# Attention in a two-layer hybrid backbone step: values as weights with two heads on the two halves of the columns, and the softmax sums divided by a diagonal while the probabilities are turned

## What is computed

```python
def block(args):
    qn_i, qr_i = args
    s = jnp.einsum('bqhd,bkhd->bhqk', qn_i, kn) + jnp.einsum('bqhr,bkr->bhqk', qr_i, kr)
    p = jax.nn.softmax(s.astype(jnp.float32) * scale, axis=-1).astype(v.dtype)
    return jnp.einsum('bhqk,bkhd->bqhd', p, v)
```

```python
u = jnp.take(u_tab, i_i, axis=0)
a = jax.nn.gelu(jnp.einsum('td,thkd->thk', x_i, u))
return jnp.einsum('thk,thkd->td', a * g_i, jnp.take(v_tab, i_i, axis=0))
```

## Time and profile before

| | us |
|---|---|
| median of 3 runs | 4947.24 (4945.59 to 4952.51) |
| the profiled execution | 4941.85 |
| its span in the trace | 4939.7 |
| TensorE busy | 3914.8 (79%) |
| VectorE busy | 3459.5 (70%) |
| ScalarE busy | 868.6 (18%) |
| GpSimd busy | 1660.4 (34%) |
| attention of "p", layer 0 | about 160 to 204 |
| attention of "s", layer 0 | about 626 to 744 |
| attention of "p", layer 1, among V | about 1829 to 1936 |
| attention of "s", layer 1 | about 2944 to 3058 |

### The profile page before, as it was taken

One profiled execution on the slowest core, in us unless ns is written; L12 is line 12 of the kernel. 1 busy time (PEld: TensorE's weight loads), 2 busy tenths in 40 slices (PEclk: granted clock), 3 DMA queues, 4 the chain that ended last, 5 costly groups with the idle time before them and its releaser, 6 DMA issues.

```text
span 4939.7 us, 40296 instructions
## 1 busy us (share of the span) xinstructions
PE 3914.8 (79%) x12034; PEld 1996.6 (40%) x12034; DVE 3459.5 (70%) x9184; ACT 868.6 (18%) x2434; POOL 1660.4 (34%) x1437
## 2 busy tenths in 40 slices
PE   7888789697988866767867579799797777777776
PEld 3437464345433333323533246445442333232322
DVE  0333788857888867777677878877787777766665
ACT  1221241001111112211111123100111111111111
POOL 0230132332233334444433323224134444443432
PEclk9879899899999988889989789999999889999999
DMA  7325377765699999999999766767479999999998
GB/s 269 117 80 197 144 273 264 268 259 214 249 376 421 407 366 402 412 409 398 417 414 421 290 231 249 300 231 274 169 266 396 406 413 411 405 415 421 417 421 347
DMA packets 223333, 1585.71 MB, mean 321 GB/s; under 512 B 26678, under 2 KB 29026, under 8 KB 32012
## 3 DMA queue, kind: packets, MB, share of 16 engines
q0 software_dynamic: 186784, 1354.97, 68.5%
q1 hardware_dynamic: 36332, 228.18, 12.0%
HBM read 1571.74 MB, written 11.30 MB: 320 GB/s over the span
## 4 chain that ended last, share of the span: by engine, by line
PE 37%; DMA 29%; DVE 22%; issue 6%; ACT 3%; POOL 3%; SPq 0%; DVEq 0%; ACTq 0%; POOLq 0%
DMA sb_gbufs<-in_peer_uv,sb_idx 16%; PE ps L1105 13%; DMA sb_arena<-in_peer_uv,sb_idx 11%; PE ps L1004 7%; DVE sb_gbufs L1863 5%; PE ps L1042 3%; DVE sb_arena L1863 3%; DVE sb_eacc L1886 2%; PE ps L674 2%; PE ps L719 2%; PE ps L688 2%; POOL sb_gbufs L2106 1%; PE ps L1022 1%; PE ps L862 1%; PE ps L1075 1%
## 5 line engine op out<-in xcount | busy, mean ns | idle before, releaser
L2106 POOL DMA_INDIRECT sb_gbufs<-in_peer_uv,sb_idx x768 | 940.5, 1225 | 1864.4 <-PE ps L1105 826.8
L1105 PE MATMUL ps<-sb_arena,sb_dge 128*128 128x512 f32 x1856 | 925.2, 649 | 301.6 <-ACT sb_dge L1368 301.4
L1105 PE MATMUL ps<-sb_gbufs,sb_dge 128*128 128x512 f32 x1856 | 907.6, 638 | 304.8 <-ACT sb_dge L1368 304.7
L2106 POOL DMA_INDIRECT sb_arena<-in_peer_uv,sb_idx x512 | 563.8, 1101 | 869.3 <-PE ps L1105 830.9
L1863 DVE CUSTOM_DVE_ANT_0 sb_gbufs<-sb_gbufs,sb_keep 128x1024 f32<-128x1024 f32 x512 | 621.4, 1226 | 289.5 <-DMA sb_gbufs<-in_peer_uv,sb_idx 288.0
L1863 DVE CUSTOM_DVE_ANT_0 sb_arena<-sb_arena,sb_keep 128x1024 f32<-128x1024 f32 x512 | 619.5, 1223 | 262.8 <-DMA sb_arena<-in_peer_uv,sb_idx 261.3
L1105 PEld LDWEIGHTS ps<-sb_arena,sb_dge 128*128 128x128 f32 x1856 | 367.9, 206 | 821.5 <-ACT sb_dge L1368 421.6
L1105 PEld LDWEIGHTS ps<-sb_gbufs,sb_dge 128*128 128x128 f32 x1856 | 362.4, 203 | 814.3 <-issue 426.7
L1363 ACT ACTIVATE sb_small<-sb_small 128x2 f32<-128x2 f32 x512 | 104.0, 203 | 2182.4 <-DVE sb_small L1874 2182.4
L1886 DVE SCALAR_TENSOR_TENSOR sb_eacc<-sb_gbufs,sb_small,sb_eacc 128x1024 f32<-128x1024 f32 x299 | 388.2, 1298 | 9.2 <-DVE sb_small L1897 0.3
L1368 ACT ACTIVATE sb_dge<-sb_ident,sb_small 128x128 f32<-128x128 f32 x928 | 327.3, 395 | 122.5 <-DVE sb_small L1960 121.8
(11 more groups left out here) (257 smaller groups left out, 4307.6 us busy)
## 6 DMA issues: line engine op xcount, KB each, us to landing
sb_ring<-in_w_ada SPq DMA_DIRECT2D x48, 1024.0 KB, 8.9
sb_ring<-in_w_wq SPq DMA_DIRECT2D x32, 1024.0 KB, 6.3
sb_ring<-in_w_hy SPq DMA_DIRECT2D x24, 1024.0 KB, 7.5
sb_ring<-in_w_ga SPq DMA_DIRECT2D x16, 1024.0 KB, 8.0
sb_ring<-in_w_gb SPq DMA_DIRECT2D x16, 1024.0 KB, 9.5
sb_ring<-in_w_oab SPq DMA_DIRECT2D x16, 1024.0 KB, 7.8
sb_ring<-in_w_out SPq DMA_DIRECT2D x14, 1024.0 KB, 9.0
sb_gbufs<-in_peer_uv,sb_idx POOLq DMA_INDIRECT x768, 11.0
```

The lines of the kernel that those rows point to most:

```text
L1105: q = pe.matmul(ps[:, c, :], dge[:, b, :], gbuf[b][:, D + c * 512:D + c * 512 + 512], start=(h == 0 and i == 0), stop=(h == HALVES - 1 and ...
L2106: nc.gpsimd.indirect_dma_start(out=gbuf[b], out_offset=None, in_=I["peer_uv"], in_offset=bass.IndirectOffsetOnAxis(ap=idx[:, col:col + 1], ...
```

## The change

The diagonal. For each head VectorE takes the reciprocal of the row sums and multiplies the identity by it (`inverse_sums`, in `rdiag`, two buffers). TensorE multiplies `prob`, as weights, by this diagonal instead of transposing it: the product is the turned probabilities, divided already. `normalise` goes. `inverse_sums(i-1)` stands at the start of VectorE's step i, ahead of the maximum of head i, and TensorE's turning(i-1) waits for it (semaphore `rd` instead of `prob`).

The values as weights. Two heads are multiplied at every second step: 64 value columns of each as weights, the turned probabilities (128 columns) moving, the even head's result on PSUM partitions 0 to 63 and the odd one's on 64 to 127. The result stands turned, so the four blocks are copied to `attnT` by ScalarE straight from the bank (`heads_done`), and the turning at L841 and its copy go. `probT` has four buffers instead of two.

The pace of a head step is 4.0 instead of 4.5. The E units that stand among the 32 head steps of "s" fall from 54 to 49 in layer 0 and from 50 to 46 in layer 1; of the nine, two go ahead of the attention, and of the seven behind it three stand among the gate products (L1004).

```diff
-        at = [20 * k] + [10] * nt + [15] + [8] * nt + [8, 10] + [4.5] * (NH * nt) + [10] + [8 * k + 2] * (8 if self.latent else 12)
+        at = [20 * k] + [10] * nt + [15] + [8] * nt + [8, 10] + [4.0] * (NH * nt) + [10] + [8 * k + 2] * (8 if self.latent else 12)
...
                         m.then_inc(s["s_ps"], 1)
+                    if i >= 3 and i % 2:
+                        j, h = (i - 3) // NH, (i - 3) % NH
+                        b = g.head_bank(j)
+                        if h == 0:
+                            claim(b, *at("aT", j + 1))
+                        pe.wait_ge(*at("pT", i - 1))
+                        for kt in range(g.nk):
+                            for u in (0, 1):
+                                m = pe.matmul(ps[64 * u:64 * u + VD, b, h * 64:h * 64 + 128], v.V[:, kt, (h + u) * VD:(h + u + 1) * VD],
+                                              v.probT[:, (i - 3 + u) % 4, kt * 128:kt * 128 + 128],
+                                              start=(kt == 0), stop=(kt == g.nk - 1), skip_group_check=True)
+                        m.then_inc(s["o_ps"], 1)
                     if 1 <= i <= N:
-                        pe.wait_ge(*at("prob", i))
+                        pe.wait_ge(*at("rd", i))
                         claim(4, *at("pT", i))
                         for kt in range(g.nk):
-                            m = pe.transpose(psf[:, 4 * 512 + kt * 128:4 * 512 + kt * 128 + 128],
-                                             v.prob[:, (i - 1) % 2, kt * 128:kt * 128 + 128], ident[:, :])
+                            m = pe.matmul(psf[:, 4 * 512 + kt * 128:4 * 512 + kt * 128 + 128], v.prob[:, (i - 1) % 2, kt * 128:kt * 128 + 128],
+                                          v.rdiag[:, (i - 1) % 2, :], start=True, stop=True)
                         m.then_inc(s["trp"], 1)
-                    if i >= 2:
...
                 vacate()
-                for j in range(nt):
-                    claim(g.lo(j), *at("aT", j + 1))
-                    pe.wait_ge(*at("attn", j + 1))
...
+                def heads_done(j):
+                    act.wait_ge(*at("o_ps", NH // 2 * (j + 1)))
+                    act.activation(v.attnT[:, :, j * 128:j * 128 + 128], ps[:, g.head_bank(j), :].rearrange("p (c t) -> p c t", c=4), ACT.Copy).then_inc(s["aT"], 1)
...
-                def normalise(j):
...
+                def inverse_sums(i):
+                    dve.wait_ge(*at("prob", i + 1))
+                    if i >= 2:
+                        dve.wait_ge(*at("trp", i - 1))
+                    link(dve.reciprocal(ssum[:, 32 + i % 2:33 + i % 2], ssum[:, i:i + 1]))
+                    dve.tensor_scalar(v.rdiag[:, i % 2, :], ident[:, :], ssum[:, 32 + i % 2:33 + i % 2], None, ALU.mult).then_inc(s["rd"], 1)
 
                 for i in range(nt * NH):
+                    if i:
+                        inverse_sums(i - 1)
                     dve.wait_ge(*at("s_ps", i + 1))
```

47 lines of the change are left out of this document (13 added, 34 removed).

## The result

| | before | after |
|---|---|---|
| median, first comparison (4 runs each) | 4949.33 us | 4994.26 us (4990.45 to 5007.05) |
| ratio, first comparison | | 1.0096, 95% interval 1.0075 to 1.0116 |
| median, second comparison (14 and 5 runs) | 4949.79 us | 4995.19 us (4983.79 to 5005.71) |
| ratio, second comparison | | 1.0080, 95% interval 1.0067 to 1.0094 |
| profiled execution, its span | 4941.85, 4939.7 us | 4990.45, 4988.6 us |

The change costs 45 us. Forecast were 4965 and a range of 4943 to 4990. The direction was right; the size is two and a half times the +18 of the forecast, and the row of rival 2 (+43, 4990) is the nearest. The page of the kernel after: PE 3924.7 us busy (before 3914.8), DVE 3484.7 (3459.5), ACT 869.5 (868.6). TensorE has 10 us more work and VectorE 25.

A forecast was written before the change was run, and what follows sets the result against it. VectorE was taken to bound the attention of "s", strict engine order phase 0, DMA phase 1. "s" 2 x (3.4 + 2.2 + 3 - 3) = +11.2, phase 0 +6, phase 1 +2: +19, 4961 profiled, 4965 median; range 4943 to 4990.

The forecast's parts named there:

- rival 2: Each stall in phase 1 costs DMA time, 26 us (seven at 3.7) instead of 2: +43, 4990; chance 0.13.
- Phase 1: Attention of "p" among V: turning waits for VectorE's next head step, V's matmuls 6.9 us later, seven times; +2 us.
- So I take +2: one loss at the first stall: Phase 1: queued gathers cover later stalls, so delays don't add up; +2 us, bounds 0 and 34.
- The moved units: Nine E units leave the head steps of "s": -0.23 and -0.18 us per step, +2.2 us a layer elsewhere.
- VectorE sets the pace there, and E units are what fills it: Attention of "s" before the change: VectorE's counted step, 3.38 and 3.19 us, matches the measured paces.
- three land among the gate products, where TensorE is busy for 186 of 200 us and VectorE for 141: free: Three of the nine moved units cost nothing; half of the other six count, +2.2 us a layer.
- VectorE's step in "s": Inverse adds 0.42 us, `normalise` and units go: 3.46 and 3.33 us a head step, +3.4 us a layer.
- forecast 2.2 us a pair: TensorE in "s": 20 value instructions one behind the other at 0.11 us, nothing gained; a step is 3.33 us.
- Rival 1: Column halves run side by side, values of "s" take 1.1 us a pair: +8 us, 4955; chance 0.27.
- The bound of 5 us a layer on the changes of weight width: TensorE in "s": 32 changes between full-width and 64-column weights a layer cost at most 5 us.
- The end of "s": Last maximum to convolution: 12.8 us becomes 10.6 or 8.5 at the half clock; -3 us a layer taken.
- Phase 0: Attention of "p": inverse and turning stand before F's matmuls, +0.8 us at six places, +1 at the end; +6 us.

The follow-up runs named there:

- before_pace: The kernel before with the pace of a head step at 4.0, nothing of the attention changed: 4964.41 us, ratio 1.0025.
- pace_back: The changed kernel with the pace of a head step at 4.5 again: 4977.49 us, ratio 1.0044.
- both_back: The changed kernel with inverses of "p" in VectorE's own step and the pace at 4.5: 4949.28 us, ratio 1.0002.
- p_own_step: The changed kernel with the inverse of "p" made in VectorE's own step, right behind the same head's maximum: 4973.05 us, ratio 1.0039.
- late_s_new: both_back with 5 and 4 E units moved from ahead of the h2 step to behind it: 4935.35 us, ratio 0.9967.
- att45_rest40: p_own_step with E units dealt as by pace 4.5 in the attention of "s", as by 4.0 elsewhere: 4971.22 us, ratio 1.0047.
- both_no_inverse: both_back without inverse and diagonal in "s" (division left out), turning by the constant identity: 4942.77 us, ratio 0.9990.
- both_transposes: both_no_inverse with the turning of "s" as 5 transposes instead of 5 products of two passes: 4938.94 us, ratio 0.9978.
- both_in_turn: both_back with a pair's value instructions one head after the other instead of alternating: 4964.31 us, ratio 1.0038.
- att40_rest45: p_own_step with E units as by pace 4.0 in the attention of "s", 4.5 elsewhere, leftovers in the following convolution: 4959.59 us, ratio 1.0024.
- before_pace50: The kernel before with the pace of a head step at 5.0: 4959.02 us, ratio 1.0016.

## Why the prediction was wrong, step by step

**Phase 1 (forecast +2 us, measured +12 in the trace and 15 to 16 in the medians).** The place and the cause of the waits were seen rightly, their length less so: 6.9 us each were expected, the trace has 8 of 38.6 us in all, 4.8 on average, the longest 9.2. What failed is the sentence "So I take +2: one loss at the first stall", with the reason that the queue before the DMA is short once and then stays so. The windows show the contrary: the DMA is back at 420 to 424 GB/s after a stall and falls again with the next, 12.6 us in all, so each of seven costs about 1.8 us of transfer. Rival 2 had it that each stall costs; its 3.7 us each are twice the measured, and its condition, a queue that doesn't refill, was not measured. TensorE's granted clock in 1841 to 1941 is 0.78 (0.89 before), which rival 2 named too; no run separates what it adds. The bounds (0 to 34) held; with 12.6 in place of 2 the forecast would have been 4976.

**The moved units (forecast -8 us in all, measured +15 by before_pace and +17 by pace_back).** The forecast has them in two terms: -0.23 and -0.18 us in VectorE's step, which is 12.7 us for 31 steps in two layers, and +2.2 us a layer for where they go. Three things failed. First, "VectorE sets the pace there, and E units are what fills it": in before_pace the steps take 3.33 and 3.28 us against 3.36 and 3.23, so nothing came back. In the new attention it was 0.16 and 0.12 (from pace_back to the change), 0.13 and 0.00 (from both_back to p_own_step). Second, "three land among the gate products, where TensorE is busy for 186 of 200 us and VectorE for 141: free": VectorE's mean share says nothing on who is late at the end of the stretch. That is the h2 step, where TensorE waited 21.6 us for VectorE already, and this wait isn't in the prediction. Units taken from ahead of it give time back (late_s_new). Third, a pace is no count of nine: it deals all 260 units anew, and att45_rest40 shows that the arrangement outside the attention alone makes the h2 wait 29.4 us. With +15 in place of -8 beside the 12.6 of phase 1 the forecast would have come out at 4999, near the 4994 measured.

**VectorE's step in "s" (forecast 3.46 and 3.33 us, measured by the scores 3.53 and 3.56).** The inverse was right to 0.02 us. With the units of before (both_back) the step grows by 0.34 and 0.30 us, forecast 0.31. What was missing is the gain from fewer units, above. both_no_inverse and both_transposes show that a step is neither VectorE's nor TensorE's alone: each shortens it.

**TensorE (forecast 2.2 us a pair, measured 1.31).** Rival 1 was right on the mechanism and wrong in its sum, because the terms for phase 1 (it has 0) and for the units were the ones that failed. TensorE's time isn't free in the new step either: 0.35 us a step more cost 15 us in both_in_turn, of which the steps show 11. The bound of 5 us a layer on the changes of weight width held; what they cost is in the last section.

**The end of "s" (forecast -3 us, measured -6.0 in layer 0 and -4.8 in layer 1).** The chain of waits after the change, from the last maximum to the convolution:

```profile
739.51 0.82 DVE sb_nmax L1565
740.33 1.19 DVE sb_eacc L1884
741.63 0.30 DVE sb_arena L1556
741.98 1.38 PE ps L832 x10
743.38 0.71 ACT sb_arena L1192
744.14 1.34 PE ps L824 x20
745.50 0.61 ACT sb_keep L1196
746.11 0.24 issue
746.35 5.82 PE ps L857 x13
```

6.8 us instead of 12.8. In layer 0 the steps are those of the forecast, but the forecast took the clock over from the old end, where it was granted at half, 1.2 GHz. Windows of the change and then of before (the seventh figure is the granted clock):

```profile
740.00:746.30 6.30, 3.71 (x40) 3.10 (x38) 4.63 (x12) 2.87 (x6) 1.35 (x2) 1.00 0.81 300
...
735.00:740.00 5.00, 4.25 (x21) 4.07 (x20) 0.67 (x2) 0.70 (x1) 0.00 (x0) 0.50 0.82 326
```

At 2.4 GHz and on the two halves in turn 20 value products take 1.34 us, where they took 4.17. TensorE's busy share in the attention ahead is the same, 86% in both. What differs just ahead of the fall is a wait: before, TensorE stood idle for 2.2 us until 733.79, with the clock at 0.87 from 730 to 735 and at 0.50 after; in the change no wait from 733 to 746 is longer than 0.95 us, and the clock stays at 1.00. Whether that is why wasn't tested.

**Phase 0 (forecast +6 us).** F's matmuls start 0.77 us after its last VectorE step (0.95 forecast):

```profile
190.12 0.68 DVE L1475 TENSOR_TENSOR sb_gbufs<-ps,sb_gbufs 128x512 f32<-128x512 f32 x1
...
191.57 3.60 PE L687 MATMUL ps<-sb_arena,sb_gbufs 128*128 128x512 f32 x8
```

From 160 to 200 the trace falls back by 7.9 us (2.1 to 10.0), within the 4 to 8 of the forecast. By 400 it is only 1.2 us late, but that is no cover for the delay: p_own_step, which has no such delay, gains as much in that stretch and is 8.9 us ahead of the kernel before at 450. Something in the new kernel gains 7 to 9 us there that the forecast doesn't have; no run isolates it. p_own_step is 10 to 11 us ahead of the change from 400 to 740. Of these, 7 go between 740 and 820, where its waits for ScalarE at L687 and for VectorE at L889 are each 2 us longer, and 1 to 4 are left from there to phase 1. The medians say 6.5.

**What stays open.** The arrangement of the units makes the h2 waits longer (7.5 and 7.9 us of the change's 45), but by what step, when their number hardly changes, isn't shown. Nor are the single steps of the 10 us between 3100 and 3450, which come in pieces of 3 to 5 us at waits for L1594, for a weight and at the gates; att45_rest40 shows them too, so they belong to the arrangement. Why 5.0 costs the new attention 30 us and the old one 8 stays open; only the head steps were measured (3.79 and 3.26 us in before_pace50). What the new attention of "p" gains between 200 and 400 is open too.

## What to carry to other kernels

Where engines run a list in different orders, ask for each new wait in which piece of the other engine's own order the releaser stands; a wait that crosses such an offset can cost up to a whole piece each time, and the stretch bound by DMA paid here for every one of them, not once. Filler work isn't free because its engine has a low busy share: here it was on the path ahead of the next wait for that engine, and moving it across the longest such wait gave 14 to 18 us. When a change carries a retuned number along, time the number alone first; here it was a third of the loss.

## What was not expected of the hardware

Products on the two halves of the columns, alternating: 20 instructions (64-column weights, 128 moving columns, float32) in 1.31 us; the same with ten for one half and then ten for the other: 2.02 us. Where full-width weights follow 64-column ones (L824 to L832) or the other way round (L813 to L824), the next product starts no sooner than 0.20 us after the last, in all 72 such places of the change, while between two full-width products (L832 to L813) it is 0.11. So each of the 32 changes a layer costs TensorE some 0.09 us, about 3 us a layer. In float32 VectorE's product of the 128x128 identity by a column lasts 0.286 us, but its successor starts 0.21 us after it.
